# Three entries of a fused three-model kernel: where ScalarE applies a gate's function, and the order of two splits

## The reference, cut to what matters

```python
def second_block(x, ...):
    h = x
    for layer in range(DEPTH_2):                 # 2 layers
        y = rms_norm(h, norm_g[layer])           # the entries "ev" and "od" of the kernel
        ...
        if layer % 2 == 0:
            h = h + even_mixer(y, ...)           # out = w_out(branches * silu(z)), z = y @ w_in[...]
        else:
            h = h + odd_mixer(y, ...)            # attention * silu(z), z = y @ w_in[...] + b_in
    return rms_norm(h, final_norm_g)

def third_block(x, ...):
    hn = rmsnorm(h, norm_w[i])
    proj = hn @ w_in[i]
    u_s5, z_s5, z_ssd, xBC, dt_raw = jnp.split(proj, SPLITS, axis=-1)
    y_s5 = s5_branch(u_s5, ...) * jax.nn.silu(z_s5)
    y_ssd = ssd_branch(xBC, dt_raw, z_ssd, ...)
    h = h + jnp.concatenate([y_s5, y_ssd], axis=-1) @ w_out[i]
    ...
```

## Time and profile before

| | us |
|---|---|
| median of 3 runs | 3231.41 (3228.7 to 3236.09) |
| profiled execution, its time | 3234.76 |
| its span, first to last instruction | 3232.9 |
| mean granted clock of TensorE | 0.985 |
| busy: PE / PEld / DVE / ACT / POOL | 3124.0 / 2456.1 / 1631.1 / 1146.3 / 943.3 |

### The profile page before, as it was taken

The page is one execution under the profiler, slowest core; times in us unless marked ns, Lnnn a source line. Parts: engine busy times, 40 slices in busy tenths (PEclk is TensorE's granted clock), DMA queues, the critical chain, the costliest instruction groups (busy, mean ns, idle before and its releaser), DMA issues.

```text
span 3232.9 us, 38359 instructions
## 1 busy us (share of the span) xinstructions
PE 3124.0 (97%) x15508; PEld 2456.1 (76%) x15508; DVE 1631.1 (50%) x2692; ACT 1146.3 (35%) x1946; POOL 943.3 (29%) x691
## 2 busy tenths in 40 slices
PE   8999989999989999999999999999999999999998
PEld 7776667666878888777887766678778888788877
DVE  6979651112446654232341467676646545543436
ACT  3125543112351111113341166445446432322334
POOL 2210001111416785124521212321011123443523
PEclk9999989999999999999999999999999999999999
DMA  4110001112422333113321101331011144433222
GB/s 133 46 33 20 14 14 42 43 40 73 168 68 86 87 92 97 49 46 136 119 95 40 41 25 60 124 100 34 27 46 47 54 120 120 131 137 111 98 76 107
DMA packets 251202, 242.25 MB, mean 75 GB/s; under 512 B 15377, under 2 KB 198033, under 8 KB 250001
## 3 DMA queue, kind: packets, MB, share of 16 engines
q1 hardware_dynamic: 230384, 197.10, 20.0%
q10 hardware_dynamic: 20640, 42.70, 3.8%
HBM read 201.03 MB, written 38.73 MB: 74 GB/s over the span
## 4 chain that ended last, share of the span: by engine, by line
PE 87%; DVE 6%; ACT 4%; DMA 1%; POOL 1%; issue 1%; SPq 0%; ACTq 0%; POOLq 0%; DVEq 0%
PE psum L555 23%; PE psum L557 22%; PE psum L556 22%; PE psum L561 4%; PE psum L675 3%; PE psum L722 1%; PE psum L748 1%; DVE arena L2835 1%; PE psum L1191 1%; PE psum L859 1%; PE psum L1142 1%; PE psum L1141 1%; DMA arena<-in_w_in 1%; PE psum L924 1%; POOL WS L3135 1%
## 5 line engine op out<-in xcount | busy, mean ns | idle before, releaser
L3135 POOL TENSOR_TENSOR WS<-arena,WS 128x1024 fp32r<-128x1024 f32 x271 | 674.6, 2495 | 1893.3 <-ACT WS L1207 1893.2
L555 PE MATMUL psum<-XH,WS 128*128 128x512 f32 x2464 | 987.7, 401 | 28.1 <-DVE XL L2231 11.1
L557 PE MATMUL psum<-XH,WS 128*128 128x512 f32 x2464 | 963.3, 391 | 0.0
L556 PE MATMUL psum<-XL,WS 128*128 128x512 f32 x2464 | 963.1, 391 | 0.0
L555 PEld LDWEIGHTS psum<-XH,WS 128*128 128x128 f32 x2464 | 464.7, 189 | 146.4 <-issue 18.2
L557 PEld LDWEIGHTS psum<-XH,WS 128*128 128x128 f32 x2464 | 464.4, 188 | 98.9
L556 PEld LDWEIGHTS psum<-XL,WS 128*128 128x128 f32 x2464 | 465.2, 189 | 95.8 <-issue 4.8
L1207 ACT ACTIVATE WS<-arena 128x1024 fp32r<-128x1024 f32 x271 | 284.6, 1058 | 677.4 <-PE psum L557 249.2
L555 PE MATMUL psum<-WS,XH 128*128 128x512 f32 (+1 forms) x1024 | 398.0, 389 | 21.0 <-DVE XL L2158 7.2
L556 PE MATMUL psum<-WS,XH 128*128 128x512 f32 (+1 forms) x1024 | 393.4, 384 | 0.0
L557 PE MATMUL psum<-WS,XL 128*128 128x512 f32 (+1 forms) x1024 | 393.3, 384 | 0.0
(11 more groups left out here) (295 smaller groups left out, 3219.2 us busy)
## 6 DMA issues: line engine op xcount, KB each, us to landing
arena<-in_w_in SPq DMA_DIRECT2D x85, 512.0 KB, 3.8
arena<-in_w_out SPq DMA_DIRECT2D x48, 512.0 KB, 3.5
arena<-in_w_in_even SPq DMA_DIRECT2D x48, 512.0 KB, 4.2
arena<-in_w_out_even SPq DMA_DIRECT2D x32, 512.0 KB, 3.3
h_spill<-arena ACTq DMA_DIRECT2D x24, 512.0 KB, 3.1
arena<-s_table SPq DMA_DIRECT2D x8, 1536.0 KB, 6.7
arena<-in_w_in_odd SPq DMA_DIRECT2D x18, 512.0 KB, 3.8
s_table<-arena SPq DMA_DIRECT2D x32, 256.0 KB, 3.0
```

Source lines behind the costliest of these rows:

```text
L555: e.matmul(ps, wh, xh, start=start, stop=False)
L556: e.matmul(ps, wh, xl, start=False, stop=False)
L557: return e.matmul(ps, wl, xh, start=False, stop=stop)
L3135: e.tensor_tensor(lo, raw(book.raw_of.get(("w", u), 0), kbs, n), hi.bitcast(F32), SUB).then_inc(*w.up("w_lo", u))
```

## The change

Three places are edited. In ev, ACT evicts the four gates of half 0 as plain copies (event z2_raw, which also frees their PSUM banks), and applies Silu to all four in place in SBUF after the turn of half 1. In od, the two gates of half 0 that come before the turn are evicted with their bias alone (Identity, event z2o_raw) and get Silu in place after the turn, ahead of the load of the positions. The third gate of od, whose half 0 comes after the turn, stays as it was. At the end of the S5 branch ACT splits half 0 of y between its evictions of the two halves of zproj(7), where both splits stood behind both evictions; DVE does its part of that split inside `mid(7)`, behind the scans and ahead of the four operations that make h5. POOL, SP and PE keep their rows in their order.

```diff
-    "b2_evac": "z2 u2 gc2 k2 z2o ksw q2",
+    "b2_evac": "z2_raw z2o_raw z2 u2 gc2 k2 z2o ksw q2",
...
             proj_first([(("z2_ps", 8 + m - m % 2, m % 2), w2[:, 5120 + 128 * m:5248 + 128 * m],
-                         lambda half, m=m: [("z2", 8 + m - m % 2, m % 2, half)]) for m in range(4)],
+                         lambda half, m=m: [("z2", 8 + m - m % 2, m % 2, 1) if half else ("z2_raw", m)]) for m in range(4)],
...
-                       [(("z2o_ps", m), w2[:, 1280 + 128 * m:1408 + 128 * m], lambda half, m=m: [("z2o", m, half)])
-                        for m in range(3)], "od", lambda: turn_half("od", xs, 1), 3)
+                       [(("z2o_ps", m), w2[:, 1280 + 128 * m:1408 + 128 * m], lambda half, m=m: [
+                           ("z2o_raw", m) if m < 2 and not half else ("z2o", m, half)]) for m in range(3)], "od", lambda: turn_half("od", xs, 1), 3)
...
-            first = [lambda half, m=m: z_ev(8 + m - m % 2)(m % 2, half) for m in range(4)]
-            weave((proj_first(first, lambda: turn_half("ev", 1, lambda kb: col("norm_g_2", kb), [("o1_ps", 1, 7)]), 4), 1, True),
+            def z_first(half, m):
+
+                if half:
+                    return z_ev(8 + m - m % 2)(m % 2, 1)
+                w.wait_ge("z2_ps", 8 + m - m % 2, m % 2, 0)
+                e.activation(OUT[:, 8 + m, half_of(0)], ps_of("z2_ps", 8 + m - m % 2, m % 2, 0), ACT.Copy).then_inc(
+                    *w.up("z2_raw", m))
+
+            def ev_turn():
+                turn_half("ev", 1, lambda kb: col("norm_g_2", kb), [("o1_ps", 1, 7)])
+                w.wait_ge("z2_raw", 3)
+                for m in range(4):
+                    o = OUT[:, 8 + m, half_of(0)]
+                    e.activation(o, o, ACT.Silu).then_inc(*w.up("z2", 8 + m - m % 2, m % 2, 0))
+            first = [lambda half, m=m: z_first(half, m) for m in range(4)]
+            weave((proj_first(first, ev_turn, 4), 1, True),
                   (ln_half(1), 2, True))
...
+            def zo_first(half, m):
+
+                if half or m == 2:
+                    return z_ev(m, half)
+                w.wait_ge("z2o_ps", m, 0)
+                e.activation(Z2[:, m, half_of(0)], ps_of("z2o_ps", m, 0), ACT.Identity,
+                             bias=col("b_in_odd_2", 10 + m)).then_inc(*w.up("z2o_raw", m))
+
             def od_turn():
                 turn_half("od", 1, lambda kb: col("norm_g_2", 8 + kb), [("x_used", "o2_ps", 1, 1, 1, 3)])
+                w.wait_ge("z2o_raw", 1)
+                for m in range(2):
+                    o = Z2[:, m, half_of(0)]
+                    e.activation(o, o, ACT.Silu).then_inc(*w.up("z2o", m, 0))
                 w.wait_ge("h_out", "od", 7)
...
-            weave((proj_first([k_ev] + [lambda half, m=m: z_ev(m, half) for m in range(3)], od_turn, 3), 1, True),
+            weave((proj_first([k_ev] + [lambda half, m=m: zo_first(half, m) for m in range(3)], od_turn, 3), 1, True),
                   (od_norm(1), 2, True))
...
-            run(zproj(7))
+            zs = zproj(7)
+            next(zs)
             for half in range(2):
                 split_half("wo0", lambda kb: Y8[kb], half, range(8), lambda kb: [("zs_ps", 7, 0, half), ("y_in", kb)])
+                run(zs)
                 if half == 0:
                     run(proj_th())
...
-                mid(e_ + 1, lambda: back5(e_))
+                mid(e_ + 1, lambda: back5(e_), None if e_ < 6 else lambda: split_half("wo0", lambda kb: Y8[kb], 0, range(8)))
...
-            for half in range(2):
-                split_half("wo0", lambda kb: Y8[kb], half, range(8))
+            split_half("wo0", lambda kb: Y8[kb], 1, range(8))
```

## The result

| | before | after |
|---|---|---|
| median, us | 3231.41 (3228.70 to 3236.09) | 3219.10 (3214.51 to 3220.27) |
| profiled execution, us | 3234.76 | 3219.1 |
| its span, us | 3232.9 | 3217.3 |
| mean granted clock | 0.985 | 0.989 |

The ratio is 0.996 with a 95% interval of 0.9948 to 0.9972: the changed kernel is 12.3 us faster by the medians, and at least 9 us by the interval. The forecast was 3218.4. The profiled executions differ by 15.7 us, more than the medians.

What follows compares the result with a forecast made beforehand. TensorE's own work was taken to bound the kernel, 87% of the span. Stalls of 9.6 us and clock of 3.35 made 13.0, taking the profiled 3234.76 to 3221.8, or 3218.4 by the median; range 3211 to 3227.

Steps and rivals of the forecast that it cites:

- The stall's term: In ev, four table loads of 1.28 us leave ACT's path to the last scaled tile: 5.1 us gained.
- dearer switch: Rival: each table switch costs more than its row, through a hidden drain; 4 us more in ev, 3214; chance 0.02.
- The clock in ev: Low clock behind ev's stall shrinks from a loss of 2.8 us to od's 1.75: 1.1 saved, bounds 0 and 2.8.
- od: predicted 1.5 and 1.75: In od, PE's wait shrinks by 1.5 us, and the clock then stays up, saving 1.75 (bounds 0 and 2.8).
- The step on the load of the positions: In od, this load is issued behind the Silu, some 2.5 us later against PE, at no cost.
- The end: predicted 3.0 of stall and 0.5 of clock: End of S5: wo's blocks start earlier, 3.0 us, and the low clock shrinks, 0.5 us (bounds 0 and 2.8).
- POOL's slowing: End of S5: DVE working beside POOL may slow POOL's product by up to 1.2 us; taken as 0.
- The predicted wait of 4.3 us: End of S5: after three matmuls of wo, PE waits about 4.3 us for POOL's block 1, not for DVE.
- the clock gives something back in od: Answers the rival that the clock gives nothing back anywhere, leaving 9.6 or 8.4 us, 3221.8 to 3223.0; chance 0.14.
- the end gives something: Answers the rival that the S5 end gives nothing, so 3.5 us fall away, 3221.9; chance 0.07.
- the Silu are covered: Answers the rival that in-place Silu hold up PE, 3.7 us in ev, 2.5 in od, 3224.6; chance 0.08.
- no weights are held up: Answers the slower rival: at the S5 end, ACT's wait for y delays wo's weight loads, reaching 3238; chance 0.03.

Runs made afterwards that it cites:

- ev_only: The kernel before with only the change of the ev entry; median 3224.17 us, ratio 0.9977 to before.
- od_only: The kernel before with only the change of the od entry; median 3226.83 us, ratio 0.9986 to before.
- ev_filler_before: The kernel before with 40 extra matmuls on old data ahead of ev's transposes of half 1; median 3229.64 us, ratio 0.9998 to before.
- end_only: The kernel before with only the edits at the end of the S5 branch; median 3230.07 us, ratio 0.9997 to before.
- ev_filler_after: The changed kernel with 18 extra matmuls ahead of ev's transposes of half 1; median 3219.01 us, ratio 0.9968 to before.
- end_act_only: The changed kernel with DVE's split of half 0 back behind the four h5 operations; median 3219.99 us, ratio 0.9970 to before.
- pool_first: The changed kernel with POOL's weight part and blocks 1 and 5 ahead of its two h5 products; median 3215.66 us, ratio 0.9950 to before.
- best1: The changed kernel with POOL's order block 1, weight part, block 5, h5 products, and ACT's second zproj(7) eviction after y block 4; median 3212.77 us, ratio 0.9939 to before.

## Why the prediction held, step by step

**ev: predicted 5.1 of stall and 1.1 of clock, found 4.68 and 1.28 in the profiled pair.** The stall's term is 0.4 too large, and one of its four loads is why. The first, at 895.86, had made DVE's tile 1.36 us later, but it had also made it start when POOL had just ended its weight split. POOL and DVE before, and then both after:

```profile
892.46 4.76 POOL L3135 TENSOR_TENSOR WS<-arena,WS 128x1024 fp32r<-128x1024 f32 x2 [12.21 <-ACT WS L1207]
...
897.47 1.26 DVE L2414 SCALAR_TENSOR_TENSOR arena<-arena 128x1024 f32<-128x1024 f32 x1
```

```profile
890.95 4.76 POOL L3162 TENSOR_TENSOR WS<-arena,WS 128x1024 fp32r<-128x1024 f32 x2 [12.16 <-ACT WS L1207]
...
894.53 2.25 DVE L2442 SCALAR_TENSOR_TENSOR arena<-arena 128x1024 f32<-128x1024 f32 x1
```

Before, POOL was done at 897.22 and DVE's operation took 1.26 us. Now DVE starts while POOL works until 895.71, and the same operation takes 2.25: 0.99 of the first load's gain is given back at once. DVE's next operation started 12.60 us ahead of the end of half 0 before, and 13.04 ahead of it after: 0.44 gained there. The other three loads made up for some of it: between ACT's tile work at 906.97 and the restart there are 7.68 us, where 11.92 stood, so 4.24 for three loads, or 1.41 each rather than 1.28, since ACT's operations overlap by some 0.1 us when no load stands between. These two make 4.68. The drain of 1.38 us beside each load, which the Trainium skill gives ("ScalarE: Activation LUTs", What ACT_TABLE_LOAD costs), does not show here either: 1.41 is far from the page's 2.66. The rival of the dearer switch falls.

**The clock in ev** came out near its size, 1.28 for 1.1, and that is luck. The way to it was od's loss taken for ev, and in ev_only the unchanged stall of od cost 1.07 us more than in before; in od_only the unchanged stall of ev cost 1.15 less, nearly as much as the whole term. By the means of all kernels the term is 0.7 us. ev_filler_before bears out that the low clock comes from the stall and that 2.8 us was the loss of that one execution.

**od: predicted 1.5 and 1.75, measured 1.65 and 1.66.** The clock stayed up behind 1.5 us of idle time, in this kernel and in the eight others with that stall. This is the one clock term that every trace bears out. The step on the load of the positions was wrong and harmless: I had it 2.5 us later, and it was not later at all, since its issue ran ahead of the Silu.

**The end: predicted 3.0 of stall and 0.5 of clock, found 2.5 together in the profiled pair.** The structure was right: three matmuls behind zproj(7), then a wait for POOL's block 1. The stall shrank from 7.21 to 5.27, by 1.94. The term was too large by POOL's slowing, 0 in the sum and 1.07 in the trace, where 1.2 was the bound; in end_only and ev_filler_after it was 1.67, beyond the bound. Its removal in end_act_only showed that DVE's split is what slows it. The predicted wait of 4.3 us was 5.3 or 5.9 for the same reason. The rest of the 2.5, some 0.6, is clock, and again not shown as a gain: the low clock behind this stall cost 2.1 to 2.8 us in five kernels that wait 7.2 us, and 1.8 to 2.6 in four that wait 5.3 or 5.9 (the first 40 matmuls behind the stall, over their time at the full clock). Over all the kernels the end gave 1.7, half of what was forecast. That the weights would come in time was right: no wait of PE for a unit there. What I had not seen, and what cost nothing only because POOL was later still, is the PSUM bank behind ACT's delayed eviction; pool_first laid it bare as 1.55 us.

**The sum.** 13.0 was predicted, 11.8 found at the three places in the profiled pair, 12.3 by the medians, 11.5 by the parts alone. By the means over all kernels without fillers in the place measured, the three places give some 10.6: ev 5.4, od 3.6, end 1.7. All of these lie within the interval of the measured gain, 9 to 17 us, so the nearness of 3218.4 to 3219.1 is in part luck: the path and the stalls of ev and od were right, the end was half its size. The rivals: the clock gives something back in od, and elsewhere too little to be shown; the end gives something; the Silu are covered; no weights are held up. What remains unsettled is why the clock falls for longer behind the same stall in one program than in another; no run here tells that apart.

## What to carry to other kernels

An engine off the critical path whose function switches cost table loads can do the plain copy at once and the function in place behind the moment that PE waits for; look for the idle time of that engine behind the turn, and for the resource that the deferred instruction frees (here a PSUM bank). When you move an operation of DVE earlier, look at what POOL does at the new time: part of the gain of an earlier start was taken back in three places where the two came to lie side by side (DVE's tile in ev, POOL's product and DVE's scans at the end). And when a wait changes its releaser, look at that releaser's own order: here moving POOL's block ahead of products that are needed only later, with the eviction freed, shortened the end stretch by 6.2 us, more than twice what the change of this place had given. Last, one profiled execution of each kernel was not enough to size the clock's part: the same stall cost up to 1.2 us more or less in the next one.

## What the runs showed of the hardware

- DVE beside POOL. Eight scans of 128x128 took 2.63 us alone, 3.69 with POOL beside them for 1.5 us (pool_first) and 5.84 with POOL beside them for 4.0 (best1). A three-operand operation of 128x1024 took 2.25 instead of 1.26. It works both ways: POOL's product of 128x508 took 2.85 or 3.45 us instead of 1.78 beside DVE's split, though not beside DVE's h5 operations.
- A DMA issue on ACT's queue ran ahead of ACT's own work: it went out at 1671.65, while ACT's table load, which stands before it in the program, began at 1673.28.
- TensorE's clock in od stayed at 1.00 behind an idle time of 1.5 us in nine kernels and fell behind 3.2 us in four, and in ev it stayed up when filler matmuls stood in a stall of 9 us. Keeping it up in ev was worth 1.6 to 2.8 us against kernels with the old stall and 1.5 to 2.3 against those with the new one, in the trace; neither could be read in the times. How long the low clock lasted behind one and the same stall differed between executions: 29 transposes took 5.04 to 6.19 us behind the old stall of ev.
